# Hybrid attention and PEER block on one core: order of late weight loads, a GpSimd row sum, and an earlier first gather

## The chip, the core and the metric

The kernel runs on one core of a Trainium2 chip. The metric is the device time of one execution in microseconds (us). Three runs of the kernel before gave 809.62, 809.75 and 810.78 us; the median is 809.75 us.

## The reference, cut to what matters

One decoder layer on 256 tokens of width 1024, everything in float32. A vector `c` gives six modulation rows (shift, scale and gate, twice). The block runs two kinds of attention that share one input and one output projection, then a post-LayerNorm, then a PEER layer: for each token and each of 8 heads, product-key search picks 16 of 16384 experts, and each expert is one row of `peer_u` and one of `peer_v`.

```python
mod = silu(c) @ w_ada + b_ada                       # 6 rows of 1024
h = x * (1 + sc1) + sh1
qa, ka, va, qb, kb, vb = split(h @ w_in)            # each 256 x 512
ya, yb = rms_norm(moba(qa, ka, va)), rms_norm(dilated(qb, kb, vb))
x = layer_norm(ALPHA * x + (1 + g1) * (concat(ya, yb) @ w_out))
h2 = x * (1 + sc2) + sh2
q = (h2 @ w_q).reshape(T, 8, 128)
v1, i1 = top_k(q[..., :64] @ sub_keys[0].T, 16); v2, i2 = top_k(q[..., 64:] @ sub_keys[1].T, 16)
vals, pos = top_k(v1[..., :, None] + v2[..., None, :], 16)      # over the 256 sums
e = i1[pos // 16] * 128 + i2[pos % 16]; g = softmax(vals)
f = sum over 8 x 16 experts of gelu(h2 . u_tab[e]) * g * v_tab[e]
x = layer_norm(ALPHA * x + (1 + g2) * f)
```

## The kernel before, in words

**Two phases.** First all dense weights are streamed in as chunks of 128 x 4096 floats (2 MB, in halves of 1 MB): 12 chunks of `w_ada`, 6 of `w_in`, 2 of `w_out`, 2 of `w_q`. Then the experts come in 256 slots (2 token tiles x 8 heads x 16 experts). A slot is one indirect DMA issued by GpSimd ("gather"), which fetches 128 rows of 2048 floats, 1 MB, one for each token of the tile: `peer_u` and `peer_v` side by side. A slot goes through four engines: VectorE takes the dot product of the first half with h2 (line 899, function `dot`), ScalarE makes the gelu and the weight and a diagonal matrix from it (724 to 737, `weigh`), TensorE multiplies the diagonal with the second half and sums in PSUM (528, `slot`), and the last of these frees the ring place for the gather six slots later (eight from slot 42 on). A few slots are summed by VectorE in place of TensorE.

**What sets the order.** Every engine runs the list `PLAN` (lines 89 to 144) in its own program order and takes from it the steps that concern it. SyncE has its own hand-written list of loads and waits (381 to 503). The engines wait for each other by semaphores. The place in PSUM of a step follows from its place in the list: six banks are handed out in turn (`PLACE`), and a step waits until the bank's last user has been read.

**Names around the change.** `wsum c` is the sum over eight rows of chunk c of `w_ada`, each times a column of silu(c) (line 1055, VectorE). For c = 10 and 11 there is no free place of 2 MB, so their rows lie in four or three scattered tiles ("patches", in `patches`): chunk 11 has rows 0 and 1 in half of `xT_y`, row 2 in `V_x1`, row 3 in `diag` and rows 4 to 7 in `H_s`; chunk 10 has rows 0 and 1 in `QT_h2T`, 2 and 3 in `hT_yT`, 4 to 7 in `H_s`. `wsuma` sums rows 0 to 3 (with a third number: two of them), `wsumb` rows 4 to 7. `patch_read` counts these parts; SyncE waits for it before it overwrites a patch with the rest of the query weights (`load_part`). `modrow` spreads a finished row over all partitions on TensorE (610) and `madd` copies it into `mod`. `rows2` folds the LayerNorm gain and offset into the rows sh2 and sc2 (1113 to 1117). `xa` and `ln1a` (t = 0) add the gated output projection of token tile 0 to x (874, 1108, 1130), `ln1b` forms h2 (882 to 893), `hT` transposes it (660), `q1 h` and `q t i` make the queries of one head or a pair of heads (517), `s1` and `s` their scores (686, 693). `wo t g n` is a part of the output projection, `v g t` the value projection of one attention group and token tile (599).

**Search.** `piece h j` is step j of 12 of the top-16 search of head h on VectorE. For head 0 `early` takes a short way: the top 8 of each side, the 64 sums, the top 8 of these, and thus the first eight expert numbers (1158 to 1175, then 993 in `hand_over`); the other eight follow with pieces 1 to 11. From piece 3 on head 0's search writes the buffer `acc[2]`, after `modrow 6` has read it, and from piece 8 on it writes `acc[3]`, after `modrow 7` has read it (`filled(dve, ("modrow", 7))` in `places_of`). The softmax weights `g_all`, without which no slot can be weighed, come in piece 11.

**First gathers.** The first six go to ring places whose weights must have been read: places 0 and 1 after `v 1 1`, 6 and 7 after `q 0 1`, 4 after half of `v 0 1`, 5 after all of it (`empty`, line 1206).

Of the kernel before, what the change touches and what calls it, by code (L numbers as in the profile page):

```python
# [1292 lines left out]
```

## Time and profile before

| | us |
|---|---|
| median of 3 runs | 809.75 |
| the profiled execution, its own time | 807.5 |
| its span from first to last instruction | 805.7 |
| TensorE busy | 682.6 (85%) |
| VectorE busy | 580.9 (72%) |
| ScalarE busy | 348.5 (43%) |
| GpSimd busy (issuing gathers) | 298.3 (37%) |
| HBM traffic | 323.74 MB, mean 402 GB/s |

The span counts from the first instruction to the last on the core; the execution's own time is 1.8 us longer. Busy TensorE time includes matmuls that only fill time between gathers, so its share alone says little. The DMA share counts how much of the time the core's 16 DMA engines had packets in work. The gathers carry 268.45 MB of the 323.74 MB. The kernel's last output rests on the last gather, and a gather can be issued only when its expert numbers are there and its ring place is free.

### The profile page before, as it was taken

To read this page: it belongs to the slowest core of one execution; us is meant where nothing else is said; L and a number is where in the kernel's file an instruction comes from. 1 tells how busy PE (TensorE), PEld (TensorE's weight loads), DVE (VectorE), ACT (ScalarE), POOL (GpSimd) and SP (SyncE) were. 2 spreads that over 40 slices of the span, in tenths; PEclk is the share of its full clock that TensorE was granted. 3 is DMA by queue.
4 is the path that set the end of the run, shared out by engine and by line. 5 is a ranking of instruction groups with operands and counts; after the bars stand their busy time and mean duration, and the time that the engine had idled before them with its cause. 6 is when DMAs were issued, how large, how long until landed. Compare 5 with 4: busy or idle time off the path is not lost.

```text
span 805.7 us, 7335 instructions
## 1 busy us (share of the span) xinstructions
PE 682.6 (85%) x1988; PEld 325.9 (40%) x1988; DVE 580.9 (72%) x1351; ACT 348.5 (43%) x999; POOL 298.3 (37%) x264
## 2 busy tenths in 40 slices
PE   8999998899899898887979778787878777878885
PEld 4887646355544463543323223232222222222221
DVE  4566968987878987777777878767576757674455
ACT  0013332666774744344545345434353434343333
POOL 1000001334543663645555435353434343434340
PEclk9999999999999999997989999999999999999998
DMA  9999996999999999999999999999999999999992
GB/s 297 379 399 417 413 417 228 403 403 417 396 421 421 421 421 420 421 422 420 422 421 423 420 423 422 421 421 421 421 422 421 421 422 421 421 422 420 421 417 115
DMA packets 57357, 323.74 MB, mean 402 GB/s; under 512 B 6178, under 2 KB 16738, under 8 KB 21218
## 3 DMA queue, kind: packets, MB, share of 16 engines
q0 software_dynamic: 37296, 268.45, 80.4%
q1 hardware_dynamic: 18994, 53.50, 17.3%
q10 hardware_dynamic: 1026, 1.32, 0.5%
q8 instruction: 16, 0.26, 0.1%
q14 instruction: 25, 0.20, 0.1%
HBM read 322.18 MB, written 1.07 MB: 401 GB/s over the span
## 4 chain that ended last, share of the span: by engine, by line
DMA 48%; PE 29%; DVE 7%; ACT 7%; issue 4%; SPq 3%; POOL 2%; DVEq 0%; POOLq 0%; ACTq 0%
DMA ring<-in_experts,e_all 42%; PE bank L528 19%; PE bank L550 5%; DVE ring L899 3%; DMA x<-in_x 3%; PE bank L517 2%; SPq L401 2%; DMA ring<-in_experts,e_last 2%; ACT diag L737 1%; DMA ring<-in_w 1%; POOL ring L1222 1%; ACT L724 1%; ACT weight L728 1%; DVE acc L1055 1%; PE bank L599 1%
## 5 line engine op out<-in xcount | busy, mean ns | idle before, releaser
L528 PE MATMUL bank<-ring,diag 128*128 128x512 f32 x956 | 471.8, 630 | 103.7 <-ACT diag L737 99.4
L1222 POOL DMA_INDIRECT ring<-in_experts,e_all x253 | 288.0, 1138 | 481.0 <-PE bank L528 292.8
L528 PEld LDWEIGHTS bank<-ring,diag 128*128 128x128 f32 x956 | 173.7, 196 | 379.5 <-ACT diag L737 210.0
L899 DVE CUSTOM_DVE_ANT_0 ring<-ring,T_h 128x1024 f32<-128x1024 f32 x128 | 156.7, 1225 | 109.3 <-DMA ring<-in_experts,e_all 106.8
L899 DVE CUSTOM_DVE_ANT_0 ring<-ring,h 128x1024 f32<-128x1024 f32 x128 | 156.6, 1224 | 63.6 <-DMA ring<-in_experts,e_all 60.7
L724 ACT ACTIVATE gel<-pre 128x1 f32<-128x1 f32 x256 | 51.8, 202 | 307.4 <-DVE pre L899 306.4
L737 ACT ACTIVATE diag<-consts,weight 128x128 f32<-128x128 f32 x239 | 95.9, 401 | 7.8
L728 ACT ACTIVATE weight<-gel,g_all 128x1 f32<-128x1 f32 x256 | 75.4, 295 | 9.3
L1055 DVE SCALAR_TENSOR_TENSOR acc<-ring,cact,acc 128x512 f32<-128x512 f32 x56 | 42.1, 752 | 4.3 <-DMA ring<-in_w 2.1
L550 PE MATMUL bank<-hT_yT,lnw 128*128 128x256 f32 x128 | 30.4, 396 | 0.9 <-DVE hT_yT L1020 0.9
L724 ACT ACT_TABLE_LOAD x23 | 29.5, 1283 | 0.4
L599 PE MATMUL bank<-ring,hT_yT 128*128 128x512 f32 x64 | 28.3, 594 | 0.7 <-DMA ring<-in_w 0.7
L550 PEld LDWEIGHTS bank<-hT_yT,lnw 128*128 128x128 f32 x128 | 25.3, 199 | 5.1 <-DMA lnw<-in_w 0.9
L771 ACT ACTIVATE QT_h2T<-bank 128x512 f32<-128x512 f32 x4 | 2.4, 597 | 52.0 <-PE bank L550 52.0
L899 DVE DVE_READ_ACCUMULATOR2_ANT pre<- 128x1 f32 x256 | 21.2, 83 | 0.0
L718 ACT ACT_TABLE_LOAD x16 | 20.5, 1283 | 0.3
L912 DVE SCALAR_TENSOR_TENSOR T_h<-ring,weight,T_h 128x1024 f32<-128x1024 f32 x16 | 20.5, 1280 | 0.0
L599 PEld LDWEIGHTS bank<-ring,hT_yT 128*128 128x128 f32 x64 | 12.0, 190 | 16.0 <-issue 15.9
L1055 DVE SCALAR_TENSOR_TENSOR acc<-H_s,cact,acc 128x512 f32<-128x512 f32 x22 | 16.5, 752 | 1.1 <-DVE acc L1055 0.2
L789 ACT ACTIVATE probs<-probs,negmax 128x128 f32<-128x128 f32 (+1 forms) x32 | 14.1, 443 | 6.7 <-DVEq L1084 6.6
L550 PE MATMUL bank<-hT_yT,ring 128*128 128x256 f32 x64 | 15.2, 383 | 0.0
L550 PE MATMUL bank<-hT_yT,H_s 128*128 128x256 f32 x64 | 14.5, 379 | 0.0
(197 smaller groups left out, 568.6 us busy)
## 6 DMA issues: line engine op xcount, KB each, us to landing
ring<-in_w SPq DMA_DIRECT2D x16, 1024.0 KB, 14.3
H_s<-in_w SPq DMA_DIRECT2D x7, 1024.0 KB, 14.3
ring<-in_w SPq DMA_DIRECT2D x12, 512.0 KB, 10.7
ring<-in_w SPq DMA_DIRECT2D x16, 256.0 KB, 6.6
lnw<-in_w SPq DMA_DIRECT2D x4, 1024.0 KB, 17.7
ring<-in_experts,e_all POOLq DMA_INDIRECT x253
H_s<-in_w SPq DMA_DIRECT2D x5, 512.0 KB, 8.8
lnw<-in_w SPq DMA_DIRECT2D x4, 512.0 KB, 8.6
```

The source lines that it names most:

```text
L401: sp.dma_start(dst[:, rows, here], src[:, rows, there]).then_inc(done, 16)
L528: last = nc.tensor.matmul(tile_sum(t)[n], diag[:, m % DIAGS, :], ring[:, RING_AT[i], D + CH * n:D + CH * n + CH], start=(s == 0), stop=(s ...
L550: last = nc.tensor.matmul(dst[:, T * j:T * j + T].rearrange("p (t c) -> p t c", t=NT), w[:, k, P * (2 * i + j):P * (2 * i + j) + P], hT[:, ...
L599: last = nc.tensor.matmul(dst[:], hT[:, k, t, :], w[:, k, :], start=(k == 0), stop=(k == KC - 1))
L718: nc.scalar.activation(bexp[:], bdiff[:], ACT.Exp, accum_out=bsum[:, 0:1]).then_inc(bexp_ready, 1)
L724: own.then(nc.scalar.activation(gel[:, r:r + 1], pre[:, r:r + 1], ACT.Gelu))
L728: ins = nc.scalar.mul(weight[:, r:r + 1], gel[:, r:r + 1], g_all[:, i:i + 1])
L737: nc.scalar.mul(diag[:, m % DIAGS, :], ident, weight[:, r:r + 1]).then_inc(diag_ready, 1)
L899: nc.vector.tensor_tensor_reduce(ring[:, r, 0:D], ring[:, r, 0:D], h2[i // SLOTS], 1.0, 0.0, ALU.mult, ALU.add, pre[:, i % PAIR:i % PAIR + ...
L912: ins = nc.vector.scalar_tensor_tensor(dve_sum, values, weight[:, r:r + 1], dve_sum, ALU.mult, ALU.add)
L1055: ins = nc.vector.scalar_tensor_tensor(part, row, cact[:, k:k + 1], before, ALU.mult, ALU.add)
L1222: nc.gpsimd.indirect_dma_start(ring[:, r, :], None, A["experts"], bass.IndirectOffsetOnAxis(ap=e_all[:, i:i + 1], axis=0)).then_inc(slot_i ...
```

## The change

**SyncE's loads.** Behind the first half of the first `w_out` chunk, the order was: three patches of chunk 11 (1 MB together), half 0 of `out 1`, half 1 of `out 0`, the first patch of chunk 10 (0.5 MB), x (1 MB), half 1 of `out 1`. It becomes: half 0 of `out 1`, half 1 of `out 0`, x, half 1 of `out 1`, then the three patches of chunk 11, then the first patch of chunk 10. What follows is as before.

**Chunk 11 on GpSimd.** The sum of rows 0 to 3 moves from VectorE (`wsuma 11`, four instructions) to GpSimd, ahead of its gathers, as four multiplications in place and four additions. VectorE adds rows 4 to 7 after a wait for the new semaphore `scaled_read`.

**VectorE's plan.** `rows2` moves ahead of `xa 0`.

**Values split.** `v 1 1` is cut into `va 1 1` (5 of 8 steps, before `ln1b`) and the rest (3 steps, behind the first scores). `v 0 1` moves ahead of `modrow 7`; `q 0 1` ahead of `q1 1`; the scores of head 1 behind `modrow 7`.

**First gather alone.** `early` finds the eight indices of both sides first and writes expert number 0 (the best of both sides is the best sum) by itself, so gather 0 waits for one column and gathers 1 to 7 for the other seven.

```diff
-READ_HIGH, READ_LOW, READ_ALL = 3, 4, 5
+READ_HIGH, READ_LOW, READ_ALL = 2, 3, 4
...
-       ("yT", 0, 1), ("wo", 0, 0, 1), ("wsuma", 10, 0), ("xa", 0), ("wo", 0, 1, 0), ("rows2",), ("wo", 0, 1, 1), ("ln1a", 0),
+       ("yT", 0, 1), ("wo", 0, 0, 1), ("wsuma", 10, 0), ("rows2",), ("xa", 0), ("wo", 0, 1, 0), ("wo", 0, 1, 1), ("ln1a", 0),
...
+VA_STEPS = 5
...
             load(("out", 0), (0,))
+            filled(sp, ("qk", 3, 1))
+            load(("out", 1), (0,))
+            load(("out", 0), (1,))
+            sp.dma_start(x[:], A["x"].rearrange("(t p) c -> p t c", p=P)).then_inc(x_in, 16)
+            load(("out", 1), (1,))
             sp.wait_ge(hT_ready, KC)
             for i in range(3):
                 load_patch(11, i)
-            filled(sp, ("qk", 3, 1))
-            load(("out", 1), (0,))
-            load(("out", 0), (1,))
             filled(sp, ("S", 3))
             load_patch(10, 0)
-            sp.dma_start(x[:], A["x"].rearrange("(t p) c -> p t c", p=P)).then_inc(x_in, 16)
-            load(("out", 1), (1,))
...
+                    split = VA_STEPS if ("va", g, t) in PLAN else 0
-                    for k in range(KC):
+                    for k in range(split) if kind == "va" else range(split, KC):
...
                 elif kind == "vcopy":
-                    act.wait_ge(patch_read, 1)
+                    act.wait_ge(scaled_read, 1)
...
+                    if step == ("wsumb", 11):
+                        dve.wait_ge(scaled_read, 1)
...
                     own.settle()
+                    for z in range(2):
+                        own.then(nc.vector.max_index(i16[:, z, 0:n], v16[:, z, 0:n], both[:, z, :]))
+                    own.settle()
+                    nc.vector.scalar_tensor_tensor(e_all[:, 0:1], i16[:, 0, 0:1], float(NK), i16[:, 1, 0:1], ALU.mult, ALU.add).then_inc(e_ready, 1)
...
-                    hand_over(0, slice(0, n))
+                    hand_over(0, slice(1, n))
...
+            own = Steps(pool, sem("pool_step"))
+            part = acc[:, 3, :]
+            pool.wait_ge(rows_in, 16)
+            pool.wait_ge(cact_ready, 1)
+            filled(pool, ("modrow", 3))
+            for k in range(KC // 2):
+                i, r = patch_of[11][k]
+                row = patches[11][i][:, r, :]
+                if r == 0:
+                    pool.wait_ge(patch_in[11][i], 16)
+                own.then(nc.gpsimd.tensor_scalar(row, row, cact[:, k:k + 1], None, ALU.mult))
+                own.settle()
+                ins = nc.gpsimd.tensor_tensor(part, row, part if k else mod[:, G2, CH:], ALU.add)
+                if k < KC // 2 - 1:
+                    own.then(ins)
+            ins.then_inc(scaled_read, 1)
-            empty = {0: [("v", 1, 1)], 6: [("q", 0, 1)], 4: [("v", 0, 1)], 2: [("wo", 1, g, 0) for g in range(2)]}
+            empty = {0: [("v", 1, 1)], 6: [("q1", 1)], 4: [("v", 0, 1)], 2: [("wo", 1, g, 0) for g in range(2)]}
...
-                if i == TOPK // 2:
-                    pool.wait_ge(e_ready, 2)
+                if i in (1, TOPK // 2):
+                    pool.wait_ge(e_ready, 2 if i == 1 else 3)
```

VectorE's program before, from the first rows of chunk 10 (`acc<-QT_h2T`) to the end of `rows2`; `ystat` opens `xa`, the three `128x1024` rows are `rows2`:

```order
L1055 SCALAR_TENSOR_TENSOR acc<-QT_h2T,cact,mod 128x512
L1055 SCALAR_TENSOR_TENSOR acc<-QT_h2T,cact,acc 128x512
L1100 RECIPROCAL ystat<-ystat 128x2
L874 SCALAR_TENSOR_TENSOR acc<-bank,ystat,mod 128x512
L1108 SCALAR_TENSOR_TENSOR x<-x,acc 128x512
L874 SCALAR_TENSOR_TENSOR acc<-bank,ystat,mod 128x512
L1108 SCALAR_TENSOR_TENSOR x<-x,acc 128x512
L1113 TENSOR_TENSOR H_s<-H_s,mod 128x1024
L1115 TENSOR_TENSOR mod<-mod,H_s 128x1024
L1117 TENSOR_TENSOR mod<-mod,H_s 128x1024
```

The same stretch after the change:

```order
L1061 SCALAR_TENSOR_TENSOR acc<-QT_h2T,cact,mod 128x512
L1061 SCALAR_TENSOR_TENSOR acc<-QT_h2T,cact,acc 128x512
L1119 TENSOR_TENSOR H_s<-H_s,mod 128x1024
L1121 TENSOR_TENSOR mod<-mod,H_s 128x1024
L1123 TENSOR_TENSOR mod<-mod,H_s 128x1024
L1106 RECIPROCAL ystat<-ystat 128x2
L878 SCALAR_TENSOR_TENSOR acc<-bank,ystat,mod 128x512
L1114 SCALAR_TENSOR_TENSOR x<-x,acc 128x512
L878 SCALAR_TENSOR_TENSOR acc<-bank,ystat,mod 128x512
L1114 SCALAR_TENSOR_TENSOR x<-x,acc 128x512
```

`rows2` now stands between the two rows of chunk 10 and `xa`; the two rows of chunk 10 lead in both.

TensorE's program before, from `v 1 1` (`bank<-ring,hT_yT`) over the transposes of h2 (`h_0`), the queries (`xT_y,ring`), scores (`skT,acc`) and modulation rows (`acc,ones`) to `v 0 1` and the first slot (`ring,diag`):

```order
L599 MATMUL bank<-ring,hT_yT 128x512 x8
L660 MATMUL bank<-consts,h_0 128x128 x8
L517 MATMUL bank<-xT_y,ring 128x128 x8
L686 MATMUL bank<-skT,acc 128x128 x2
L610 MATMUL bank<-acc,ones 128x512
L517 MATMUL bank<-xT_y,ring 128x128 x8
L686 MATMUL bank<-skT,acc 128x128 x2
L517 MATMUL bank<-xT_y,ring 128x128 x16
L610 MATMUL bank<-acc,ones 128x512
L599 MATMUL bank<-ring,hT_yT 128x512 x8
L528 MATMUL bank<-ring,diag 128x512 x2
```

And after:

```order
L602 MATMUL bank<-ring,hT_yT 128x512 x5
L664 MATMUL bank<-consts,h_0 128x128 x8
L519 MATMUL bank<-xT_y,ring 128x128 x8
L690 MATMUL bank<-skT,acc 128x128 x2
L602 MATMUL bank<-ring,hT_yT 128x512 x3
L614 MATMUL bank<-acc,ones 128x512
L519 MATMUL bank<-xT_y,ring 128x128 x24
L602 MATMUL bank<-ring,hT_yT 128x512 x8
L614 MATMUL bank<-acc,ones 128x512
L690 MATMUL bank<-skT,acc 128x128 x2
L530 MATMUL bank<-ring,diag 128x512 x2
```

The last `acc,ones`, which is `modrow 7`, stood ahead of the eight matmuls of `v 0 1` and now stands behind them; three of the eight of `v 1 1` have moved behind the first scores.

## Rows read from the trace of the kernel before

**Rows 1.** The page, part 2: HBM traffic in 40 equal slices of 20.1 us.
```profile
GB/s 297 379 399 417 413 417 228 403 403 417 396 421 421 421 421 420 421 422 420 422 421 423 420 423 422 421 421 421 421 422 421 421 422 421 421 422 420 421 417 115
```

**Rows 2.** Windows: busy us of each engine, then clock, DMA share, GB/s.
```profile
127.50:131.50 4.00, 3.13 (x19) 2.15 (x18) 3.65 (x5) 1.56 (x3) 0.00 (x0) 1.00 0.10 43
137.00:140.00 3.00, 2.64 (x23) 2.55 (x24) 2.83 (x7) 0.65 (x3) 1.55 (x2) 1.00 0.03 12
140.00:152.50 12.50, 11.71 (x40) 5.82 (x39) 11.54 (x46) 6.30 (x14) 4.77 (x6) 1.00 0.97 368
152.50:169.00 16.50, 14.81 (x53) 7.59 (x52) 14.75 (x45) 13.72 (x36) 5.15 (x5) 1.00 1.01 425
169.00:181.00 12.00, 11.38 (x36) 5.80 (x34) 8.84 (x34) 6.07 (x17) 5.20 (x5) 1.00 0.98 390
```

**Rows 3.** Timeline of SyncE's DMA issues: start us, us, transfer.
```profile
92.54 0.36 SPq L455 DMA_DIRECT2D QT_h2T<-in_w  x1
...
92.95 2.13 SPq L468 DMA_DIRECT2D x<-in_x  x1
...
101.43 0.33 SPq L455 DMA_DIRECT2D hT_yT<-in_w  x1
```

**Rows 4.** DMA issues, 85 to 150 us: count, KB each, median us to landing.
```profile
x<-in_x SPq DMA_DIRECT2D x1, 1024.0 KB, 22.9
...
QT_h2T<-in_w SPq DMA_DIRECT2D x2, 512.0 KB, 20.7
...
hT_yT<-in_w SPq DMA_DIRECT2D x2, 512.0 KB, 18.1
```

**Rows 5.** Timeline of VectorE: start, us, line, shape, [idle before, its releaser].
```profile
113.48 0.75 DVE L1055 SCALAR_TENSOR_TENSOR acc<-QT_h2T,cact,mod 128x512 f32<-128x512 f32 x1 [3.03 <-DMA QT_h2T<-in_w]
...
115.83 0.17 DVE L1100 RECIPROCAL ystat<-ystat 128x2 f32<-128x2 f32 x1 [0.81 <-DMA x<-in_x]
...
118.88 1.22 DVE L1113 TENSOR_TENSOR H_s<-H_s,mod 128x1024 f32<-128x1024 f32 x1
...
122.54 0.74 DVE L874 SCALAR_TENSOR_TENSOR acc<-bank,ystat,mod 128x512 f32<-128x512 f32 x1
...
134.53 0.49 DVE L928 MAX8 v<-H_s 128x8 f32<-128x128 f32 x2 [0.64 <-ACT H_s L745]
...
137.69 0.17 DVE L993 SCALAR_TENSOR_TENSOR e_all<-eij 128x8 int32<-128x8 f32 x1
...
145.59 0.42 DVE L983 TENSOR_TENSOR acc<-pij,consts 128x256 f32<-128x256 uint32 x1
...
147.81 1.21 DVE L899 CUSTOM_DVE_ANT_0 ring<-ring,h 128x1024 f32<-128x1024 f32 x1
...
150.16 1.23 DVE L899 CUSTOM_DVE_ANT_0 ring<-ring,h 128x1024 f32<-128x1024 f32 x1 [0.34 <-DMA ring<-in_experts,e_all]
...
153.50 1.23 DVE L899 CUSTOM_DVE_ANT_0 ring<-ring,h 128x1024 f32<-128x1024 f32 x1 [0.71 <-DMA ring<-in_experts,e_all]
```

**Rows 6.** Timeline of TensorE, between the first queries and slot 0.
```profile
137.87 3.84 PE L517 MATMUL bank<-xT_y,ring 128*128 128x128 f32 x32
...
141.55 1.02 PE L610 MATMUL bank<-acc,ones 128*128 128x512 f32 x2
...
142.41 7.03 PE L599 MATMUL bank<-ring,hT_yT 128*128 128x512 f32 x16
```

**Rows 7.** Timeline of GpSimd: gathers 0, 6 and 11.
```profile
138.14 1.34 POOL L1222 DMA_INDIRECT ring<-in_experts,e_all  x1 [133.89 <-DVE e_all L993]
...
152.46 0.94 POOL L1222 DMA_INDIRECT ring<-in_experts,e_all  x1 [1.81 <-PE bank L528]
...
169.11 1.30 POOL L1222 DMA_INDIRECT ring<-in_experts,e_all  x1 [2.90 <-PE bank L528]
```

**Rows 8.** Timeline of GpSimd at the start of the program.
```profile
0.74 3.51 POOL L1205 MEMSET mod<- 128x4096 f32 x1 [0.29 <-POOLq L1282]
```

**Rows 9.** A window after TensorE went idle at 408.6 us.
```profile
410.00:412.00 2.00, 0.00 (x0) 0.00 (x0) 2.00 (x3) 0.76 (x3) 0.69 (x1) 0.77 1.02 426
```

More of the change, by code:

```diff
@@ L102 @@
        ("qk", 3, 1), ("modrow", 2), ("madd", 2), ("wsum", 8), ("S", 2), ("S", 3), ("modrow", 3), ("madd", 3), ("wsum", 9), ("v", 1, 0),
[4 rows of a table removed]
-    + [("piece", 0, 0), ("early",), ("wsumb", 11), ("q1", 1), ("s1", 1, 0), ("s1", 1, 1), ("q", 0, 1), ("modrow", 7)] + [("piece", 0, j) for j in range(1, EXP_PIECE)] + [("v", 0, 1)]
[4 rows of a table added]
+    + [("piece", 0, 0), ("early",), ("wsumb", 11), ("q", 0, 1), ("q1", 1), ("v", 0, 1), ("modrow", 7), ("s1", 1, 0), ("s1", 1, 1)] + [("piece", 0, j) for j in range(1, EXP_PIECE)]
     + [("piece", 0, j) for j in range(EXP_PIECE, PIECES)] + AFTER_HEAD0
@@ L153 @@
 OPENED = [("qk",) + s[1:] for s in PLAN if s[0] == "qkz"]
-FILLS = OPENED + [s for s in PLAN if s[0] not in NO_FILL and s not in OPENED]
+BEGUN = {("va",) + s[1:]: s for s in PLAN if s[0] == "v" and ("va",) + s[1:] in PLAN}
+FILLS = OPENED + [BEGUN.get(s, s) for s in PLAN if s[0] not in NO_FILL and s not in OPENED and s not in BEGUN.values()]
 APART = [("bias",)] + [("modc", h) for h in range(QUARTERS)] + [("wo", 0, 1, n) for n in range(2)]
@@ L297, in build @@
         v_half = sem("v_half")
-        patch_read = sem("patch_read")
+        patch_read, scaled_read = sem("patch_read"), sem("scaled_read")
         patch_in = {c: [sem(f"patch_in{c}_{i}") for i in range(len(patches[c]))] for c in patches}
@@ L579, in _ @@
                     continue
-                if step in OPENED:
+                if step in OPENED or step in BEGUN.values():
                     dst, full = bank[PLACE[step][0]], bank_full[PLACE[step][0]]
                 else:
-                    dst, full = open_bank(step)
+                    dst, full = open_bank(BEGUN.get(step, step))
                 if kind == "bias":
@@ L601, in _ @@
                             last.then_inc(v_half, 1)
-                    last.then_inc(full, 1)
+                    if kind == "v":
+                        last.then_inc(full, 1)
                 elif kind == "lnb":
@@ L995, in hand_over @@
                 if head == NT * PH - 1:
-                    dve.wait_ge(e_ready, NT * PH + 1)
+                    dve.wait_ge(e_ready, NT * PH + 2)
                     last = e_all[:, ENDING[0]:NT * SLOTS]
@@ L1157, in _ @@
                     own.settle()
+                    for z in range(2):
+                        own.then(nc.vector.max_index(i16[:, z, 0:n], v16[:, z, 0:n], both[:, z, :]))
+                    own.settle()
+                    nc.vector.scalar_tensor_tensor(e_all[:, 0:1], i16[:, 0, 0:1], float(NK), i16[:, 1, 0:1], ALU.mult, ALU.add).then_inc(e_ready, 1)
                     own.then(nc.vector.tensor_tensor(sums.rearrange("p (i j) -> p i j", i=n), v16[:, 0, 0:n].unsqueeze(2).broadcast_to(square),
                                                      v16[:, 1, 0:n].unsqueeze(1).broadcast_to(square), ALU.add))
-                    own.then(nc.vector.max_index(i16[:, 0, 0:n], v16[:, 0, 0:n], both[:, 0, :]))
                     own.settle()
                     own.then(nc.vector.max(best[:, 0:n], sums))
-                    own.then(nc.vector.max_index(i16[:, 1, 0:n], v16[:, 1, 0:n], both[:, 1, :]))
                     own.settle()
@@ L1209, in _ @@
                 if i % TOPK == 0:
-                    pool.wait_ge(e_ready, i // TOPK + min(i, 1) + 1)
-                if i == TOPK // 2:
-                    pool.wait_ge(e_ready, 2)
+                    pool.wait_ge(e_ready, i // TOPK + 2 * min(i, 1) + 1)
+                if i in (1, TOPK // 2):
+                    pool.wait_ge(e_ready, 2 if i == 1 else 3)
                 if i in ENDING:
```

2 lines of the change are left out of this document (1 added, 1 removed), and 6 rows, old and new, of the table PLAN.

## The prediction

> **What bounds the kernel now.** I began with the page's line of HBM traffic: from the tenth slice on it stands at 420 to 423 GB/s, but for the last slice, so the gathers run as fast as memory gives, and the end can move only by what the DMA engines do not carry somewhere. Three places are below that: the first slices, the last, and slice 7, near 121 to 141 us, with 228 GB/s [rows 1]. The change touches only slice 7. Windows over it show two holes, 127.5 to 131.5 us (43 GB/s) and 137 to 140 us (12 GB/s), then 368 GB/s up to 152.5 us [rows 2]. In the first hole all weights that had room were loaded and SyncE waited for VectorE; the second lasts until gather 0, issued at 138.14 us [rows 7], moves bytes, about 2 us later (140 us in the windows).
>
> Then I asked whether the compute behind the gathers has slack. By the issue of gather 6 at 152.46 us [rows 7], six gathers and one 1 MB weight piece (7.34 MB) were issued, and 12.5 us x 368 GB/s = 4.6 MB moved: 2.7 MB or 6.5 us waited. By gather 11 (169.11 us) 12.6 MB were issued and 4.6 + 16.5 x 0.425 = 11.6 MB moved: 0.96 MB or 2.3 us, and a gather takes 2 us to start. So the cushion of 4.5 us at gather 6 is 0.3 us at gather 11, and the next 12 us run at 390 GB/s [rows 2], a loss of 12 x (1 - 390/421) = 0.9 us. Over this stretch the slots come no faster than ScalarE, VectorE and TensorE handle them between search and attention steps. A later start of slot 0 can be absorbed only as far as this cushion.
>
> Last the chain ahead of gather 0 on VectorE: wait for chunk 10's patch (113.48), wait for x (115.83), `rows2` (118.88), `ln1a` (122.54), the search (134.53), the numbers (137.69) [rows 5].
>
> **Part 1, the loads.** x goes ahead of 1.5 MB (three patches of chunk 11, one of chunk 10). At 0.42 MB per us it lands about 3.7 us sooner: 92.95 + 22.9 = 115.8 before, 112.1 after [rows 3, 4]. The patch of chunk 10, however, goes behind everything. The next transfer after it, hT_yT's patch, is untouched and lands at 101.43 + 18.1 = 119.5 [rows 3, 4]; the bytes ahead of it are the same; QT_h2T's 0.52 MB stand just ahead, so they land at 119.5 - 1.25 = 118.3, against 92.54 + 20.7 = 113.2 before: 5 us later. This rests on landings in the order of issue, which the three rows keep: 113.2, 115.8, 119.5.
>
> The Trainium skill speaks against that reading (DMA: Bandwidth & Descriptors, Queues, rings and completion order): descriptors start in ring order, but completion is not guaranteed to follow it from one DMA to another. The rows agree with order to within a transfer; if it did not hold, rival A below.
>
> **Part 2, VectorE up to the search.** `wsuma 10 0` still stands ahead of `rows2` and `xa` in the program, and VectorE goes in order. So it starts near 118.5 instead of 113.48. Its length is 1.56 us (two of 0.78), that of `rows2` 122.54 - 118.88 = 3.66, of `xa` 118.88 - 115.83 = 3.05 [rows 5]. `ln1a` starts at 118.5 + 1.56 + 3.66 + 3.05 = 126.8 instead of 122.54: +4.25 us. Early x is worth nothing, since `xa` now stands behind a later landing, and the 3.1 us of `wsuma 11` taken off VectorE lie in its wait. From `ln1a` to the search (134.53) nothing changes, so the search starts at 138.8. Splitting `v 1 1` frees TensorE ahead of the transposes, but `va` must wait for its bank until `xa` has read the first output product, about 124.8; VectorE's sums, which the scores' copy waits for, end the chain anyway. Value: 0, bounds -0.5 and +1 us.
>
> TensorE's clock is a danger there: it is idle from about 120 to 124.8. After such a pause the granted clock falls from 1.00 to 0.5, as the 0.77 mean of the window 410 to 412 us begins to show [rows 9]; half speed would cost `va` up to 4.4 us, which end before the transposes or 1 us behind them. That is the +1.
>
> **Part 3, the first gather.** From the search to the eight numbers 3.16 us passed, for twelve short instructions [rows 5]. Expert number 0 now needs four and one more: 1.4 us, so 140.2, and gather 0 at 140.5 against 138.14: +2.3 us. The other seven numbers come 0.3 us later than the chain gives.
>
> **Part 4, GpSimd.** Eight instructions on 128 x 512. Nearest rows: a fill of 128 x 4096 in 3.51 us, 0.44 us for 512 [rows 8]; VectorE's 0.75 us for one such sum [rows 5]. I take 1 us each, 8 us, between 3.5 and, were they three times VectorE's, 18 us. Patches land from 115.8 on, so it is done by 124 to 134, ahead of gather 0 at 140.5 and of `wsumb 11` at 142: nothing. What it may do to VectorE meanwhile I bound by 0 and 4 us (half of the 8) and take 0, since no row shows an interference.
>
> The Trainium skill names one (SBUF — State Buffer, SBUF: two separate sides): a VectorE instruction with two SBUF inputs and a GpSimd one that reads SBUF exclude each other for a whole instruction. No row here shows it. The Trainium skill (GPSIMD Engine Reference, Elementwise) gives 4497 ns for an addition of 2048 columns; an estimate from it is 1.1 us for 512.
>
> **Part 5, from gather 0 to slot 0.** This is the largest term. Head 0's piece 8 (145.59 us [rows 5]) waits for `modrow 7`, which ran at 141.55, ahead of `v 0 1`. Now TensorE does, from the scores at 133.74 + 4.25 = 138.0: three steps of `v 1 1`, 3/8 of 7.03 = 2.6; `modrow 6`, 0.9; 48 query matmuls at 3.84/32 = 0.12, 5.7; `v 0 1`, 6.9; `modrow 7`, 0.9 [rows 6]. That is 155.0. VectorE would be at piece 8 at 145.59 + 4.55 = 150.1 and stands for 5 us. The first dot follows piece 8 by 147.81 - 145.59 = 2.2 us: 157.3 against 147.81, +9.5. Before, dots 1 and 2 also waited 0.34 and 0.71 us for their gathers; now the data are long there, so dot 2 comes at 157.3 + 5.69 - 1.05 = 161.9 against 153.50: +8.4 us [rows 5]. Gather 6, issued 4.65 us behind dot 0, goes at 161.9 against 152.46; seven units from 142.5 last until about 160.5, so the DMA engines run dry before it, and again at gathers 9 and 11, whose ring places come free 8.4 us later.
>
> **Sum.** The chain is 8.4 us late at gather 11, of which 0.3 us of cushion and part of the 0.9 us already lost there are absorbed; I take 0.9: +7.5 us. No later edit gives any back, since the stream is full from there. Own time of the profiled execution 807.5 + 7.5 = 815.0; the median of the runs shown is 2.25 above that execution, so 817.3 us.
>
> **Rivals.**
> A: transfers do not land in order, QT_h2T's patch still by 113.5. Then x at 112 helps: `wsuma` ends at 115.0, `ln1a` starts at 121.7, -0.8 us. Part 5 stays: 8.4 - 5.05 = +3.4, less 0.9: +2.5, 812.2 us. Against it the three landings in order.
> B, the faster side: the stall at piece 8 is covered by the gathers already under way, and only the moment counts at which the stream of gathers starts. With A's landing it starts at -0.8 - 1.95 = -2.7 us: 807.0 us. For it: 6.5 us of transfers wait at gather 6. Against it: the 2.3 us left at gather 11. It decides at a stall below the cushion there, and needs slots 2 to 7 to be faster than the 2.2 us each of before.
> C: GpSimd and VectorE block each other between 118 and 127 us. The chain gains up to 4 us, I take 3: 820.3 us. For it is only that both read memory in that stretch; no row against it.
> D: all cancels; late landing and stall are hidden by the cushion and gather 0 wins little: 809 to 811 us.
>
> **How the numbers follow.** Forecast 0.55 (815 to 819), A 0.12, B 0.10, C 0.16, D 0.07. The range 811 to 821.5 leaves out B, most of D and a little of C. Within 0.2%, 1.6 us, a run cannot be told from no change: faster 0.11, same 0.07, slower 0.82.
>
> **What would show it.** VectorE idle near 110 to 118 us with QT_h2T's transfer as releaser; `rows2` from 120; gather 0 at 140.5; VectorE idle about 5 us ahead of piece 8, released by TensorE; first dot near 157; gather 6 near 162, and the windows 160 to 180 well below 421 GB/s. It is wrong if the patch of chunk 10 is there by 114 us, if piece 8 finds `modrow 7` done, or if the stream is full between 160 and 180 us.

## The result and the profile after

The changed kernel took 824.72 us (median of 4 runs, 821.55 to 831.54) against 809.68 us for the kernel before (4 runs, one more than stood above); the ratio is 1.022 (95% interval 1.0187 to 1.0252). The profiled execution took 821.55 us, 14.05 more than that of before. Slower was forecast, but 7.5 us of it. Ratios and ranges below leave out three runs in a slower state: one of experiment 11 (824.57 us, mean granted clock 0.835 against 0.96 to 0.98) and two of the kernel before.

Page part 2 of the changed kernel, HBM traffic in 40 slices of 20.5 us:

```profile
GB/s 304 376 404 411 421 415 165 328 290 380 418 389 423 414 422 420 421 422 422 419 421 422 420 423 420 422 420 421 422 421 421 422 422 421 421 422 421 422 418 132
```

The stretch that had one low slice before [rows 1] now has three, 165, 328 and 290 GB/s; from slice 13 on the two lines are alike. Windows of it, columns as in [rows 2]:

```profile
124.00:128.00 4.00, 1.51 (x2) 0.84 (x3) 3.90 (x6) 0.00 (x0) 3.92 (x3) 0.50 0.64 180
128.00:137.00 9.00, 6.36 (x17) 2.61 (x15) 8.34 (x14) 2.71 (x5) 1.97 (x2) 0.85 0.19 82
137.00:145.00 8.00, 6.79 (x26) 4.65 (x26) 5.83 (x20) 1.28 (x4) 0.00 (x0) 0.79 0.59 197
145.00:150.00 5.00, 4.97 (x38) 4.50 (x39) 4.62 (x14) 0.93 (x2) 2.34 (x2) 1.00 0.54 185
150.00:161.00 11.00, 9.66 (x36) 4.88 (x34) 4.58 (x18) 1.64 (x5) 3.74 (x4) 1.00 1.00 407
161.00:171.00 10.00, 5.98 (x12) 2.59 (x13) 8.13 (x31) 7.68 (x19) 0.94 (x1) 0.83 0.55 209
171.00:183.00 12.00, 12.00 (x47) 6.57 (x46) 11.64 (x33) 11.26 (x32) 4.00 (x4) 1.00 0.97 380
```

The first hole is longer, and a new one stands at 161 to 171 us (209 GB/s): the first six gathers had been carried and the seventh was not issued until 168.83 us. VectorE's timeline in the changed kernel:

```profile
118.21 0.87 DVE L1061 SCALAR_TENSOR_TENSOR acc<-QT_h2T,cact,mod 128x512 f32<-128x512 f32 x1 [7.38 <-DMA QT_h2T<-in_w]
...
121.78 2.17 DVE L1121 TENSOR_TENSOR mod<-mod,H_s 128x1024 f32<-128x1024 f32 x1
...
123.98 1.60 DVE L1123 TENSOR_TENSOR mod<-mod,H_s 128x1024 f32<-128x1024 f32 x1
...
132.04 0.21 DVE L1139 TENSOR_SCALAR lnst<-lnst 128x1 f32<-128x1 f32 x1
...
142.08 0.49 DVE L932 MAX8 v<-H_s 128x8 f32<-128x128 f32 x2 [1.60 <-ACT H_s L749]
...
159.34 0.43 DVE L987 TENSOR_TENSOR acc<-pij,consts 128x256 f32<-128x256 uint32 x1 [6.02 <-PE bank L614]
...
161.83 0.16 DVE L969 RECIPROCAL bsum<-bsum 128x1 f32<-128x1 f32 x1 [0.95 <-ACT bexp L722]
...
162.61 1.21 DVE L903 CUSTOM_DVE_ANT_0 ring<-ring,h 128x1024 f32<-128x1024 f32 x1
```

Four lines of the kernel before, to compare with: the second instruction of `rows2`, the mean for LayerNorm that ends `ln1a` (`lnst`), TensorE's queries of head 0, and slot 0.

```profile
120.14 1.22 DVE L1115 TENSOR_TENSOR mod<-mod,H_s 128x1024 f32<-128x1024 f32 x1
...
125.45 0.21 DVE L1133 TENSOR_SCALAR lnst<-lnst 128x1 f32<-128x1 f32 x1
...
130.69 2.02 PE L517 MATMUL bank<-xT_y,ring 128*128 128x128 f32 x16 [0.87 <-ACT xT_y L745]
...
150.23 1.96 PE L528 MATMUL bank<-ring,diag 128*128 128x512 f32 x4 [0.79 <-ACT diag L737]
```

The patch of chunk 10 was waited for until 118.2 us, to 0.3 us as forecast, and VectorE had idled 7.4 us. Then two things that I had set to nothing: the three instructions of `rows2` take 1.23, 2.17 and 1.60 us where they took 1.22 to 1.23, and the search waits 1.60 us for scores instead of 0.64. Piece 8 waits 6.02 us for `modrow 7`, and the softmax weights another 0.95 us for ScalarE. The first dot comes at 162.61 instead of 147.81. TensorE's timeline:

```profile
126.49 6.62 PE L602 MATMUL bank<-ring,hT_yT 128*128 128x512 f32 x10 [6.53 <-DVE acc L878]
...
137.11 3.41 PE L519 MATMUL bank<-xT_y,ring 128*128 128x128 f32 x16 [0.77 <-ACT xT_y L749]
...
141.51 2.84 PE L602 MATMUL bank<-ring,hT_yT 128*128 128x512 f32 x6
...
145.03 1.13 PE L614 MATMUL bank<-acc,ones 128*128 128x512 f32 x2 [0.68 <-ACT V_x L749]
...
158.22 1.02 PE L614 MATMUL bank<-acc,ones 128*128 128x512 f32 x2
...
165.02 3.54 PE L530 MATMUL bank<-ring,diag 128*128 128x512 f32 x4 [5.36 <-ACT diag L741]
```

`va 1 1` waited 6.53 us for the bank that `xa` empties, and began at the low level of the granted clock (0.50, 1.2 GHz, in the window 124 to 128 us); the eight query products took 3.41 us instead of 2.02, and slot 0 3.54 us instead of 1.96. GpSimd's:

```profile
115.62 1.57 POOL L1224 TENSOR_SCALAR xT_y<-xT_y,cact 128x512 f32<-128x512 f32 x1 [111.39 <-DMA xT_y<-in_w]
...
120.60 2.27 POOL L1226 TENSOR_TENSOR acc<-xT_y,acc 128x512 f32<-128x512 f32 x1
...
122.85 2.53 POOL L1224 TENSOR_SCALAR V_x<-V_x,cact 128x512 f32<-128x512 f32 x1
...
128.79 1.26 POOL L1226 TENSOR_TENSOR acc<-diag,acc 128x512 f32<-128x512 f32 x1
...
145.26 1.15 POOL L1246 DMA_INDIRECT ring<-in_experts,e_all  x1 [15.21 <-PE bank L602]
...
168.83 0.94 POOL L1246 DMA_INDIRECT ring<-in_experts,e_all  x1 [9.24 <-PE bank L530]
...
183.27 0.94 POOL L1246 DMA_INDIRECT ring<-in_experts,e_all  x1 [2.90 <-PE bank L530]
```

The sums last from 115.6 to 130.0 us. Against [rows 7] gather 0 is 7.1 us later, gather 6 16.4 and gather 11 14.2 us. The last number is the whole loss (14.05 us in the own time).

### The profile page after: what moved, and what is told of

Read it like the earlier page. It is cut to its first block, busy times and chain, and to the rows that moved or that the text cites. A ratio compares the mean times of both kernels' runs of the same rounds, so it can differ in the third digit from the quotient of the medians.

```text
span 819.7 us, 7341 instructions
## 1 busy us (share of the span) xinstructions
PE 685.7 (84%) x1988; PEld 325.9 (40%) x1988; DVE 580.5 (71%) x1348; ACT 349.0 (43%) x999; POOL 305.8 (37%) x272
## 4 chain that ended last, share of the span: by engine, by line
DMA 48%; PE 30%; ACT 8%; DVE 8%; issue 3%; POOL 1%; SPq 1%; DVEq 0%; POOLq 0%; ACTq 0%
DMA ring<-in_experts,e_all 42%; PE bank L530 17%; PE bank L552 6%; DVE ring L903 3%; DMA QT_h2T<-in_w 3%; PE bank L602 2%; DMA ring<-in_w 2%; PE bank L519 2%; ACT diag L741 2%; DMA ring<-in_experts,e_last 2%; ACT L728 1%; ACT weight L732 1%; POOL ring L1246 1%; DVE acc L1061 1%; ACT gel L728 1%
## 5 line engine op out<-in xcount | busy, mean ns | idle before, releaser
L1246 POOL DMA_INDIRECT ring<-in_experts,e_all x253 | 281.3, 1112 | 375.9 <-PE bank L530 298.1
L1224 POOL TENSOR_SCALAR xT_y<-xT_y,cact 128x512 f32<-128x512 f32 x2 | 3.6, 1783 | 111.4 <-DMA xT_y<-in_w 111.4
L602 PE MATMUL bank<-ring,hT_yT 128*128 128x512 f32 x64 | 30.7, 633 | 7.1 <-DVE acc L878 6.5
L552 PE MATMUL bank<-hT_yT,lnw 128*128 128x256 f32 x128 | 28.7, 380 | 0.9 <-DVE hT_yT L1024 0.9
L722 ACT ACT_TABLE_LOAD x16 | 20.5, 1283 | 0.3
L916 DVE SCALAR_TENSOR_TENSOR T_h<-ring,weight,T_h 128x1024 f32<-128x1024 f32 x16 | 20.5, 1280 | 0.0
## 6 DMA issues: line engine op xcount, KB each, us to landing
ring<-in_w SPq DMA_DIRECT2D x16, 1024.0 KB, 14.2
```

The costliest lines, as they stand in the source:

```text
L552: last = nc.tensor.matmul(dst[:, T * j:T * j + T].rearrange("p (t c) -> p t c", t=NT), w[:, k, P * (2 * i + j):P * (2 * i + j) + P], hT[:, ...
L602: last = nc.tensor.matmul(dst[:], hT[:, k, t, :], w[:, k, :], start=(k == 0), stop=(k == KC - 1))
L722: nc.scalar.activation(bexp[:], bdiff[:], ACT.Exp, accum_out=bsum[:, 0:1]).then_inc(bexp_ready, 1)
L916: ins = nc.vector.scalar_tensor_tensor(dve_sum, values, weight[:, r:r + 1], dve_sum, ALU.mult, ALU.add)
L1246: nc.gpsimd.indirect_dma_start(ring[:, r, :], None, A["experts"], bass.IndirectOffsetOnAxis(ap=e_all[:, i:i + 1], axis=0)).then_inc(slot_i ...
```

## The experiments

Ratios are to runs of the kernel before made beside each experiment, with 95% intervals; the times themselves come from several sessions and are compared through these ratios. Each trace is of one execution. The same stretch can differ between executions by 1 us and more where the edit does not touch it: the search began at 142.08 us in the changed kernel, at 142.59 in experiment 5 and at 142.99 in experiment 2. Experiments 1 to 8, 11 and 12 start from the changed kernel, 9 and 10 from the kernel before. M is the changed kernel with modrow 7 first (experiment 2).

**1. Patch 10 ahead of x.**

```diff
             load(("out", 0), (1,))
+            filled(sp, ("S", 3))
+            load_patch(10, 0)
             sp.dma_start(x[:], ...)
...
-            filled(sp, ("S", 3))
-            load_patch(10, 0)
```

> The changed kernel with one edit: the first patch of chunk 10 is loaded ahead of x, not behind the patches of chunk 11. Theory (VectorE's order makes the late patch delay rows2 and xa): the patch lands near 111 us and x near 113, ln1a starts near 120 instead of 128.7, the second centring of h2 near 125 instead of 132.4, gather 0 near 138 instead of 145.3, and 7 us of the 15 come back: about 817 us. Rival (GpSimd's sums and TensorE's clock set the start of ln1a, the patch only fills idle time): less than 2 us come back, 823 us or more.

818.27 us (815.51 to 820.67), 1.0132 (1.0076 to 1.0188). VectorE and TensorE in this kernel:

```profile
111.08 0.74 DVE L1061 SCALAR_TENSOR_TENSOR acc<-QT_h2T,cact,mod 128x512 f32<-128x512 f32 x1
...
134.88 0.49 DVE L932 MAX8 v<-H_s 128x8 f32<-128x128 f32 x2 [0.64 <-ACT H_s L749]
...
156.62 3.75 PE L530 MATMUL bank<-ring,diag 128*128 128x512 f32 x4 [5.36 <-ACT diag L741]
...
162.30 5.39 PE L530 MATMUL bank<-ring,diag 128*128 128x512 f32 x8
```

The search came 7.2 us sooner, as the theory had it, and stood within 0.35 us of the kernel before. The first dot came 8.4 us sooner (154.20). But gather 11 came only 5.6 us sooner (177.71): behind the same pause of 5.36 us the granted clock stood at 0.50 up to 165 us, through slots 0 and 1 (5.39 us for slots 1 and 2, against 3.70 in the changed kernel).

The edit did not take GpSimd's hindrance away, it moved it: `rows2` now runs ahead of GpSimd's sums and takes its old lengths, but an instruction of `ln1b` behind it takes 2.10 us instead of 1.28, and the sums of chunk 10 take 2.74 and 4.00 us instead of 1.54 and 3.11.

**2. modrow 7 first (M).**

```diff
-("q", 0, 1), ("q1", 1), ("v", 0, 1), ("modrow", 7), ("s1", 1, 0), ("s1", 1, 1)]
+("q", 0, 1), ("q1", 1), ("modrow", 7), ("s1", 1, 0), ("s1", 1, 1), ("v", 0, 1)]
```

> The changed kernel with one edit: modrow 7 and the scores of head 1 stand ahead of v 0 1 again. Theory (piece 8 of head 0 and the softmax's exp wait for what stands behind v 0 1): VectorE's 6.0 us idle ahead of piece 8 and the 0.95 us ahead of its weights go, the first dot comes near 156 instead of 162.6; slot 0 then waits for v 0 1 to end near 160, so it starts 5 us earlier and at full clock; about 6.5 us come back, 818 us. Rival (the gathers already under way cover the stall, as before): the same as the changed kernel within 2 us.

815.80 us (815.08 to 816.79), 1.0092 (1.0062 to 1.0122). VectorE and TensorE:

```profile
154.27 0.42 DVE L987 TENSOR_TENSOR acc<-pij,consts 128x256 f32<-128x256 uint32 x1
...
160.57 1.88 PE L530 MATMUL bank<-ring,diag 128*128 128x512 f32 x4
```

Piece 8 waits for nothing, slot 0 follows `v 0 1` at once and at full clock. This edit gave the most: 5.9 us of the profiled execution's 14, and the ratio from 1.022 to 1.009. That is more than the 6.5 us expected: some 10 us by the ratios.

**3. Without GpSimd's sum.**

```diff
-                own.then(nc.gpsimd.tensor_scalar(row, row, ...))
-                own.settle()
-                ins = nc.gpsimd.tensor_tensor(part, row, ...)
...
-            ins.then_inc(scaled_read, 1)
+            pool.sem_inc(scaled_read, 1)
```

> The changed kernel without GpSimd's eight instructions: rows 0 to 3 of chunk 11 are left out of the sum (that part of the gate row is not computed); waits and loads stand. Theory (GpSimd and VectorE hold each other up between 118 and 130 us): chunk 10's two sums and rows2 take their lengths of before (0.75 and 1.22 us), ln1a starts near 127 instead of 128.7 and the search 2 to 2.5 us earlier; about 2.5 us come back, 822 us. Rival (the longer times on VectorE have another cause, as the late landings): lengths and time stay.

825.97 us (820.89 to 830.91), 1.0241 (1.0177 to 1.0305): no gain. VectorE and TensorE:

```profile
121.26 1.23 DVE L1121 TENSOR_TENSOR mod<-mod,H_s 128x1024 f32<-128x1024 f32 x1
...
129.67 0.21 DVE L1139 TENSOR_SCALAR lnst<-lnst 128x1 f32<-128x1 f32 x1
...
138.75 0.49 DVE L932 MAX8 v<-H_s 128x8 f32<-128x128 f32 x2 [0.64 <-ACT H_s L749]
...
161.24 3.75 PE L530 MATMUL bank<-ring,diag 128*128 128x512 f32 x4 [5.36 <-ACT diag L741]
...
166.93 5.32 PE L530 MATMUL bank<-ring,diag 128*128 128x512 f32 x8
```

The instruction that took 2.17 us takes 1.23 again, the mean for LayerNorm comes 2.4 us earlier and the search 3.3 us, and the queries of head 0 take 2.02 us again: the hindrance is real, and the rival (another cause of the longer times) falls. But the low clock lasted into slots 1 and 2 (granted 0.50 up to 169 us), and gather 11 (182.26) gained 1.0 us. One edit alone could not show what the sum costs; experiment 7 gives an estimate.

**4. Both edits, 1 and 2.**

> Both edits: the patch of chunk 10 ahead of x, and modrow 7 with head 1's scores ahead of v 0 1. Theory (the two delays follow one another on one chain): the gains add, 7 + 6.5 us, about 811 us, still 1 to 2 us over the kernel before for GpSimd's hindrance. Rival (either delay alone is enough to fill the same hole): not more than the larger of the two alone, 817 us.

808.65 us (806.55 to 814.07), 1.0010 (0.9984 to 1.0036). The gains add, and the rival (the larger of the two alone) falls: by the ratios about 7 and 10 us alone and 17 together, in the profiled executions 5.2 and 5.9 alone and 12.4 together. With no pause ahead of slot 0, the earlier search also reaches gather 11. What is left of the change does no harm that these runs can measure (-1.3 to +2.9 us).

**5 and 6. Filling TensorE's pauses.**

```diff
+                if kind == "fill":     # cut: 6 ahead of slot 0; in the second kernel also 6 ahead of va, 4 ahead of hT
...
+                    for _ in range(step[2]):
+                        nc.tensor.matmul(dst, ones[:], ..., start=True, stop=True)
```

> The changed kernel with six filling matmuls of 128x512 (result unused) on TensorE between the scores of head 1 and slot 0, where it stood idle for 5.4 us. Theory (the pause drops the granted clock, and slots 0 to 2 run at the lower level and hold back the gathers behind them): slot 0 takes 2.0 us instead of 3.5, gather 6 goes 1.5 us earlier, gather 11 up to 3 us, 821 to 822 us and the runs lie within 3 us of each other instead of 10. Rival (slots 0 to 2 wait for ScalarE's table loads and VectorE anyway): same time, same scatter.

821.51 us (819.75 to 822.62), 1.0176 (1.0160 to 1.0193). TensorE and GpSimd:

```profile
165.50 1.96 PE L530 MATMUL bank<-ring,diag 128*128 128x512 f32 x4
...
183.13 0.94 POOL L1253 DMA_INDIRECT ring<-in_experts,e_all  x1 [2.90 <-PE bank L530]
```

Slot 0 takes 1.96 us. The profiled execution is as long as that of the changed kernel, but the runs lie within 2.9 us instead of 10, and the median is 3.2 us lower. Gather 11 at 183.13 us is where it was (183.27), but the first dot was 0.5 us later in this execution (163.09). Counted from the first dot, gather 11 came 20.66 us behind it in the changed kernel and 20.04 with the fill: there the low clock cost 0.6 us. In the profiles of experiments 1 and 3, where it lasted longer, gather 11 came 23.5 and 23.4 us behind the first dot: 3.4 us. The lower median suggests that such executions are among those of the changed kernel too; but the intervals of the two ratios (1.0160 to 1.0193, 1.0187 to 1.0252) still touch, so this is likely and not shown.

> As before, and also six such matmuls ahead of va 1 1 and four ahead of the transposes of h2. Theory: the queries of head 0 take 2.0 us instead of 3.4, VectorE waits 0.6 us instead of 1.6 for the first scores, everything behind comes 1 us earlier than with the fill ahead of slot 0 alone: about 820.5 us. Rival (the fills delay the transposes and the clock is not the cause): the same or slower than with the one fill.

821.53 us (819.39 to 823.69), 1.0188 (1.0167 to 1.0209). In its profile the queries of head 0 took 2.02 us and VectorE waited 0.64 us for the scores, as expected; the search stood at 141.21 and gather 11 at 181.34, 1.8 us earlier than with one fill. The timed runs do not tell the two apart, so what the earlier pauses cost in the median is open.

**7. M without GpSimd's sum.** The edits of 2 and 3.

> The changed kernel with modrow 7 ahead of v 0 1 (which leaves TensorE no pause ahead of slot 0), and without GpSimd's eight instructions: rows 0 to 3 of chunk 11 are left out of the sum. Theory (GpSimd's hindrance costs VectorE and what follows 3.3 us, and in the run without the sum alone this was eaten by a longer stretch of low clock in slots 0 to 2): 3.3 us below the kernel with modrow 7 first, so 812.5 us or 1.005 times before. Rival (the hindrance is real but not on the chain): the 1.009 of modrow 7 first stays.

810.88 us (810.28 to 813.08), 1.0054 (1.0037 to 1.0070), gather 11 at 172.56 against 177.16 in M. The sum on GpSimd costs 3 us by the ratios, where the two intervals just overlap (give or take 3 us, an estimate from their widths), and 4.6 us in the profiles, of which some 0.9 are M's own late search, from which its edit cannot come (142.99 against 142.08 in the changed kernel). So it is 3 to 4 us, and the rival (real but off the chain) is most likely wrong.

**8. M with xa first.**

```diff
-("wo", 0, 0, 1), ("wsuma", 10, 0), ("rows2",), ("xa", 0), ("wo", 0, 1, 0)
+("wo", 0, 0, 1), ("xa", 0), ("wsuma", 10, 0), ("rows2",), ("wo", 0, 1, 0)
```

> The changed kernel with modrow 7 first and with xa ahead of wsuma 10 and rows2 on VectorE, loads as changed (the patch of chunk 10 still lands near 118). Theory (the late patch costs what stands behind it in VectorE's program, and xa need not stand there): xa runs near 112 to 115, in the idle time; ln1a starts 3 us earlier than with modrow 7 first, near 125.5, va 1 1 follows the output product without a pause; 3 us back, ratio 1.0055. Rival (the order of xa and rows2 does not matter, only the patch's landing): 1.009 as before.

812.92 us (812.30 to 815.12), 1.0072 (1.0053 to 1.0091). `xa` ran at 112.22 us, in VectorE's idle time, and the search came 2.4 us earlier. The profiled executions differ by 3.4 us, as expected, but the ratios only by 1.6 us, with overlapping intervals: that the order of `xa` and `rows2` matters is shown in the trace and not in the timed runs. The trace also shows why less came back: TensorE, done early with `va 1 1`, stood idle for 7.96 us, and the transposes and queries behind it took 1.94 and 3.75 us where the kernel before took 1.04 and 2.02.

**9. Before with the first gather alone.**

```diff
+                    for z in range(2):
+                        own.then(nc.vector.max_index(i16[:, z, 0:n], ...))
+                    own.settle()
+                    nc.vector.scalar_tensor_tensor(e_all[:, 0:1], ...).then_inc(e_ready, 1)
...
-                    hand_over(0, slice(0, n))
+                    hand_over(0, slice(1, n))
...
-                if i == TOPK // 2:
-                    pool.wait_ge(e_ready, 2)
+                if i in (1, TOPK // 2):
+                    pool.wait_ge(e_ready, 2 if i == 1 else 3)
```

> The kernel before with only the first gather alone. Gather 0 goes near 136.2 instead of 138.1 and the seven other numbers come 0.3 us later. Theory (behind the first gathers the chain of dots and slots sets the pace, the cushion at gather 11 is 0.3 us): no gain, within 0.3% of before, rather 0.3 us slower. Rival (the moment at which the stream starts sets the end): 1.5 to 2 us faster, 0.998.

807.62 us (806.64 to 810.72), 1.0011 (1.0000 to 1.0021). GpSimd:

```profile
135.90 1.08 POOL L1224 DMA_INDIRECT ring<-in_experts,e_all  x1 [131.66 <-DVE e_all L1161]
...
167.87 1.11 POOL L1224 DMA_INDIRECT ring<-in_experts,e_all  x1 [2.90 <-PE bank L528]
```

Gather 0 went 2.2 us earlier and nothing came of it in the timed runs: slot 0 stood at 150.25 us and gather 6 at 152.47, as before. The rival (0.998) lies outside the interval and falls.

**10. Before with modrow 7 behind v 0 1.**

```diff
-("q1", 1), ("s1", 1, 0), ("s1", 1, 1), ("q", 0, 1), ("modrow", 7)] + [...] + [("v", 0, 1)]
+("q", 0, 1), ("q1", 1), ("v", 0, 1), ("modrow", 7), ("s1", 1, 0), ("s1", 1, 1)] + [...]
```

> The kernel before with only TensorE's order around v 0 1 as in the changed kernel: q 0 1 ahead of q1 1, then v 0 1, then modrow 7 and the scores of head 1. Theory (piece 8 of head 0 and the exp wait behind v 0 1, then a pause of TensorE and half clock in slots 0 to 2): VectorE idle 3 to 4 us ahead of piece 8, first dot near 153 instead of 147.8, gather 6 at 159 instead of 152.5, 5 to 8 us slower, ratio 1.006 to 1.010. Rival (the 6.5 us of transfers that wait at gather 6 cover it): same time as before.

815.11 us (812.33 to 818.32), 1.0096 (1.0066 to 1.0125). VectorE and TensorE:

```profile
149.97 0.42 DVE L983 TENSOR_TENSOR acc<-pij,consts 128x256 f32<-128x256 uint32 x1 [2.71 <-PE bank L610]
...
155.65 3.75 PE L528 MATMUL bank<-ring,diag 128*128 128x512 f32 x4 [5.37 <-ACT diag L737]
```

(GpSimd's wait for ring places 6 and 7 goes from `q 0 1` to `q1 1`, as in the changed kernel.) This reordering alone, on the kernel before, makes it 1% slower, with the wait at piece 8 and the half clock in slot 0; that the transfers in flight cover it, the rival, falls. Not all of its profile is the edit's: in this execution the granted clock also fell to 0.50 before 120 us, ahead of everything that the edit touches, and the search began at 136.26 us, 1.7 us late.

**11 and 12. A repaired version.** Edits 1 and 2, and the sum on VectorE again, between `early` and `wsumb 11`; then also `v 1 1` whole.

```diff
-    + [("piece", 0, 0), ("early",), ("wsumb", 11), ...
+    + [("piece", 0, 0), ("early",), ("wsuma", 11), ("wsumb", 11), ...
...
-       ("va", 1, 1), ("ln1b", 0), ... ("s1", 0, 1), ("v", 1, 1), ("modrow", 6)      # second kernel
+       ("v", 1, 1), ("ln1b", 0), ... ("s1", 0, 1), ("modrow", 6)
```

> The changed kernel with patch 10 ahead of x, modrow 7 ahead of v 0 1, and the sum of rows 0 to 3 of chunk 11 on VectorE again, between early and wsumb 11 (whole result computed). Theory: without GpSimd's hindrance the search starts near 132.5 (before: 134.5), gathers 0 and 1 come 2 to 4 us earlier than before, the 3.1 us of the sum lie ahead of head 0's pieces while TensorE makes v 0 1, slot 0 starts near 152 against 150.2 of before: ratio 0.998 to 1.002. Rival (only the stream's first moment counts): 0.995.

807.48 us (12 runs; 805.95 to 811.41 in all but one), 1.0003 (0.9988 to 1.0018). Search at 131.04; GpSimd:

```profile
133.77 1.08 POOL L1228 DMA_INDIRECT ring<-in_experts,e_all  x1 [129.52 <-PE bank L602]
...
168.18 0.94 POOL L1228 DMA_INDIRECT ring<-in_experts,e_all  x1 [2.90 <-PE bank L530]
```

The search came 3.5 us earlier than in the kernel before and 7.7 us earlier than in experiment 3, which also has no sum on GpSimd but the late patch. Gather 0 is 4.4 us earlier than before, slot 0 at 150.55, and the time is the same.

> As before, and v 1 1 whole ahead of the transposes of h2. Theory (the split costs TensorE 2.6 us plus a wait of 0.7 us for ScalarE's copy on its way to v 0 1, while in front of the transposes it stood idle 2 us): slot 0 starts 2 to 3 us earlier than in the kernel with the split, near 149.5, gather 0 is not held by v 1 1: ratio 0.995 to 0.998. Rival (the whole v 1 1 delays the transposes and so the search): no better than with the split.

809.98 us (807.43 to 812.08), 1.0022 (1.0006 to 1.0039). TensorE:

```profile
142.57 2.04 PE L614 MATMUL bank<-acc,ones 128*128 128x512 f32 x2 [4.39 <-DVE acc L1059]
...
145.27 9.10 PE L602 MATMUL bank<-ring,hT_yT 128*128 128x512 f32 x16
```

TensorE came to `modrow 7` too soon and stood for VectorE's sum 4.39 us. Behind that pause the granted clock was 0.50 up to 148 us, so `v 0 1` took 9.10 us instead of 7.03, and slot 0 started at 154.21 us, not at 149.5. My expectation was wrong, and the rival (no better than with the split) holds: earlier work on TensorE only made the pause. No version beat the kernel before.

**The profiles together.** Own time against the issue of gather 11, in us, for seven of the fourteen kernels:

| kernel | gather 0 | slot 0 starts | gather 11 | own time | own time less gather 11 |
|---|---|---|---|---|---|
| before | 138.14 | 150.23 | 169.11 | 807.50 | 638.4 |
| repaired (11) | 133.77 | 150.55 | 168.18 | 805.95 | 637.8 |
| edits 1 and 2 | 140.03 | 154.47 | 171.06 | 809.17 | 638.1 |
| M without sum | 141.52 | 155.96 | 172.56 | 810.89 | 638.3 |
| before, modrow 7 late | 139.86 | 155.65 | 174.61 | 814.17 | 639.6 |
| M | 146.14 | 160.57 | 177.16 | 815.69 | 638.5 |
| changed | 145.26 | 165.02 | 183.27 | 821.55 | 638.3 |

Over 15 us of spread the rest is 637.8 to 639.6 us. The other seven, not in the table, lie at 637.5 to 638.8. The end is gather 11 plus a stream, to within 2.1 us; where gather 0 stands does not matter, as the second row and the last two show.

## Why the prediction was wrong, step by step

**What bounds the kernel: right.** The stream is full behind the stretch, and a delay at gather 11 passes to the end undiminished, as the table shows. Rival B, that only the start of the stream counts, is refuted by experiments 9 and 11. (The 2.2 us that I gave there for each of slots 2 to 7 are wrong: in the kernel before, dots 2 to 7 start 2.6 us apart on average, 153.50 to 166.28 us. No term of the sum used them.)

**Part 1, the landing: right.** 118.2 us for 118.3; landings kept the order of issue, so rival A fell. Experiment 1 shows that the late patch held back the search by 7 us, more than the 4.25 forecast against the kernel before: without the late patch and the sum on GpSimd, the changed order would have brought the search forward by 3.5 us (experiment 11).

**Part 2, VectorE up to the search: right in mechanism, mis-sized.** Forecast +4.25 us, measured 142.08 - 134.53 = +7.55. The mean for LayerNorm, at 132.04 against 125.45 us, was already +6.6: 4.3 of it forecast, 2.3 from GpSimd (without its sum the mean stood at 129.67, where the forecast has it). The other 1 us is the low clock in the queries (3.41 against 2.02 us), which left VectorE waiting 1.60 us for the scores instead of 0.64. It came with GpSimd's sum: without it TensorE's pause ahead of the transposes was 1.21 us instead of 1.95, and the queries took 2.02. I had bounded the clock only for `va`, as up to +1 us, and not followed it into what comes next.

**Part 3, the first gather: right for the number, wrong for the gather, and worth nothing.** Number 0 was written 1.3 us behind the start of the search (143.4), as forecast, but gather 0 went 3.2 us behind it (145.26) and not 1.7: it was held by `v 1 1` on TensorE, whose last three steps the split put behind the scores. Experiment 9 shows that nothing hangs on it.

**Part 4, GpSimd: the value 0 was wrong; this is one step that failed.** Its eight instructions took 14 us, within my bound of 18, but they lengthened VectorE's beside them. No row of before showed an interference, and I took that for a cost of nothing. Rival C named the mechanism and priced it at 3 us; measured 2.3 us up to the mean, 3.3 us up to the search with the clock (experiment 3), and 3 to 4 us at the end (experiment 7).

The Trainium skill (SBUF — State Buffer, SBUF: two separate sides) states a lock on a shared pair of ports: of a VectorE instruction with two SBUF inputs and a GpSimd instruction that reads SBUF, the one that starts first holds the other back for its whole length. The trace agrees: `rows2`'s second instruction, with two SBUF inputs, began at 121.78 us beside GpSimd's addition, which ran until 122.87, and took 2.17 us, and 1.23 us without it. The addition itself had begun beside `rows2`'s first instruction and took 2.27 us instead of 1.26.

**Part 5, from gather 0 to slot 0: right in mechanism, mis-sized.** First dot forecast at 157.3, measured 162.61. Of the 5.3 us, 3.3 are the late search; 0.7 are a wait that I did not see (`modrow 6` takes the bank of `v 1 1`, whose copy on ScalarE now comes just ahead of it: 0.68 us at 145.03); 1.0 is the exp behind the scores of head 1 on ScalarE, since these scores had moved behind `modrow 7` with it; the remaining 0.3 us is open. I followed TensorE's queue through the change but not ScalarE's.

**Behind slot 0: a step missing.** I said that slots 0 to 5 would run as before, 8.4 us late. But the 5 us stall that I forecast on VectorE is a 5.4 us pause of TensorE, and slot 0 ran at half clock (3.54 us): gather 6 came 6.2 us behind the first dot instead of 4.65. In the profiled execution all but 0.6 us of this was made good by gather 11 (experiment 5). In the profile without the sum it cost 3.4 us there (experiments 3 and 5). I had written down the clock's fall after a pause and looked for pauses only ahead of the search.

**The sum.** The profiled execution took 14.05 us more for 7.5 forecast, and the excess of 6.5 us has these parts. 3.3 us are GpSimd's sum up to the search, set to nothing in Part 4. 2.0 us are the waits of Part 5 for ScalarE and what is open there. The rest are terms that should have given time back and gave less. From the first dot to gather 11 the forecast falls from +9.5 to +8.4; measured, it falls from +14.8 to +14.2, because the waits of dots 1 and 2 for their data went away but the low clock came (+16.4 at gather 6): 0.5 us. Behind gather 11 I let 0.9 us be absorbed; measured was 0.1 (14.16 against 14.05): 0.8 us. The median moved by 1 us more than the profiled execution, since it lies 3.2 us above it and not 2.25.

The direction and the chain held; what failed is the size of the couplings between engines: GpSimd on VectorE, pauses on TensorE's clock, the moved copies and scores on ScalarE, and a cushion behind gather 11 that was not there.

## What to carry to other kernels

When a change makes an engine wait, ask what that wait does to the clock and the queues of the others: here a wait of VectorE became a pause of TensorE and half speed behind it. Find the instruction whose moment sets the end (here gather 11, by a difference of 637.5 to 639.6 us over all fourteen kernels) and price each edit there; here an earlier first gather was worth nothing, and work moved from a waiting engine to another one cost time. Change load order and program order together: here the patch that was moved back held up all that stood behind its reader in VectorE's program.

## What the runs showed of the hardware

GpSimd's multiplication by a column (128x512, in place) took 1.57 to 2.53 us in the changed kernel, its addition of two operands 1.26 to 2.27 us, while VectorE did both at once in 0.75 us. While both engines worked, the lengths of both grew: GpSimd's addition from 1.26 to 2.27, VectorE's instructions with two SBUF inputs from 1.23 to 2.17 and, for the sums of chunk 10, from 0.75 to 1.06 us. VectorE's instructions that read one input from PSUM (`acc<-bank,ystat,mod`) kept 0.74 to 0.75 us beside GpSimd's at 125.69, 127.20 and 128.69 us.

Behind one and the same pause of 5.4 us ahead of slot 0, the stretch at the granted clock of 0.50 differed in length: slots 1 and 2 behind it took 3.70 us in the changed kernel, which is also their length with the pause filled, and 5.39 us in experiment 1.

Whether such pauses make the runs scatter is open. With the pause, the changed kernel spread over 10.0 us, the one without the sum over 10.0, experiments 1 and 10 over 5.2 and 6.0; with the pause filled, over 2.9 and 4.3; M, without a pause, over 1.7. But experiment 4, which has no pause ahead of slot 0 either, spread over 7.5 us in 10 runs, so pauses there are not the only source.
